# Six of nine modulation vectors move from TensorE to VectorE and GpSimd, their pieces loaded among the w_in and w_o chunks

## The chip, the cores and the metric

One core of one Trainium2 chip runs the whole program; everything is float32. The metric is the device time of one execution in microseconds (us). The engines are named as in the profile: PE is TensorE, DVE is VectorE, ACT is ScalarE, POOL is GpSimd, SP is SyncE, which issues nearly all loads.

## What is computed

A trunk of two layers over 256 tokens of 1024 channels. From one vector `c` each layer derives six modulation vectors of 1024 values, a shift, a scale and a gate for its mixer and the same for its expert layer:

```python
cs = jax.nn.silu(c)
for i in range(DEPTH):
    mod = cs @ w_mod[i] + b_mod[i]
    sh_m, sc_m, g_m, sh_f, sc_f, g_f = jnp.split(mod, 6, axis=-1)
    h = modulate(rmsnorm(x, norm_mix[i]), sh_m, sc_m)
    y = hybrid_ab(h, ...) if i % 2 == 0 else multiscale_pool(h, ...)
    x = x + g_m[:, None, :] * y
    h = modulate(rmsnorm(x, norm_ffn[i]), sh_f, sc_f)
    x = x + g_f[:, None, :] * hier_moe(h, ...)
return rmsnorm(x, norm_out)
```

So there are twelve vectors, called (layer, number) below: (0,0) and (0,1) are shift and scale of the first mixer, (0,2) its gate, (0,3), (0,4), (0,5) shift, scale and gate of the first expert layer, and (1,0) to (1,5) the same for the second layer. Each is a product of a 1024-vector with a 1024x1024 matrix, 4 MB of weights. The first mixer has sparse attention (an indexer, top 64 of the keys, eight heads) beside a gated spatial MLP, then the projection `w_o`; the second is a pooling mixer. The expert layer routes each token to two of 32 experts, whose weights are 96 MB per layer and are all loaded.

## The kernel before

The weights pass through `ring`, four slots of 2 MB. `plan` is the order of the 2 MB pieces: four pieces of (0,0) and (0,1), then `w_in` in the pieces qi, kv, (two pieces of (0,2)), q, v, u, then the two halves of `w_o`, then the pieces of (0,3), (0,4), (1,0) and (0,5). SP issues them in this order (L278), each when PE has used the piece four places ahead of it (`chunk_done`, one semaphore that counts pieces in PE's order). Every other load is behind it in the same queue. After the pieces come the expert weights, two experts at a time: a pair of slots holds gate and up weights, `dn_w` the down weights, and each load waits for the matmuls that read what it overwrites (L315 to L321). While the last experts of layer 0 run, the pieces of (1,1), (1,2) and then (1,3), (1,4), (1,5) are loaded.

PE computes a vector in `vector` (L446): every column of `cs` is broadcast to 32 columns of weights, so that four matmuls share the array, and a bias row is added by a matmul with a column of the identity. A gate vector then passes through ACT (`parts`, L836) and a second matmul (`gate`, L481) that sums its four parts; the others are copied to `stage` (L848) and turned on DVE (`scale_shift`, L1072). PE's order of work is written out: (0,0), (0,1), projection qi (L507), kv (L523), (0,2), key transposes (L529), indexer scores (L545), q, attention, v, the transposes of the probabilities, u, the spatial matmul (L637), values, `w_o` (L655); then `route(0)`: (0,3), (0,4), the transposes of the normed tokens (L495), the router (L667), (1,0), the counts, (0,5), the gather (L696); then the experts (L726, L738, L759, L773). After them (1,1), transposes, (1,2), the pooling mixer (L820), and `route(1)` with (1,3), (1,4), (1,5).

DVE carries the indexer: the weighted sum of the rectified scores (L1148, L1150), 8 rounds of `max` and `match_replace` per token block (L1169, L1170), then per unit of heads the distance term (L1211), mask and maximum (L1214), the division (L1226), and the GELU and layer norm of v (L1160, L1161, L1190 to L1199). ACT rectifies a unit of scores only when DVE has added the one before last (L893), copies `wsT` after the last of them (L898), and PE's projection q waits for that copy (L565). POOL has little: constants (L354 to L406), small loads, the power -1/2 of the norms (L367, L409, L411, L426), and the low parts of the tokens in `split_tokens` (L416).

## Time and profile before

| | us |
|---|---|
| median of 3 runs (776.96 to 777.67) | 777.55 |
| the profiled execution | 779.68 |
| its span from first to last instruction | 777.6 |

| engine | busy us | share of the span | instructions |
|---|---|---|---|
| PE | 679.7 | 87% | 4370 |
| DVE | 328.1 | 42% | 857 |
| ACT | 171.1 | 22% | 345 |
| POOL | 33.0 | 4% | 58 |

The chain of work that ended last is 49% PE and 44% DMA, of which 39% is `dn_w<-in_w_down`, the loads of the expert layers. The DMA engines are busy 85.5% of the span on SP's queue. A stretch that the chain gives to PE is one where PE had work without a gap; a stretch given to a DMA is one where PE stood until the load landed. Busy shares over the whole span mix stages that wait for different things, so the rows further down are read stage by stage.

### The profile page before, as it was taken

How to read it: one execution, taken by the hardware profiler on the slowest of the kernel's cores; microseconds unless marked ns; L12 is line 12 of the kernel's file. 1: busy time of each engine (PE TensorE's matmuls, PEld its weight loads, DVE VectorE, ACT ScalarE, POOL GpSimd, SP SyncE). 2: the span in 40 equal slices, each digit the busy share in tenths (PEclk: the TensorE clock that was granted, in tenths of full speed). 3: DMA queues.
4: the chain of work that ended last, by engine and by line, in shares of the span. 5: the costliest groups of instructions: out<-in, count | busy, mean ns of one | idle time of the engine just before them, and what ended most of it. 6: DMA issues, size and time to landing. Idle time of an engine off the chain costs nothing.

```text
span 777.6 us, 11606 instructions
## 1 busy us (share of the span) xinstructions
PE 679.7 (87%) x4370; PEld 386.2 (50%) x4370; DVE 328.1 (42%) x857; ACT 171.1 (22%) x345; POOL 33.0 (4%) x58
## 2 busy tenths in 40 slices
PE   4799998999998898889889879988988898898894
PEld 2285666435665444445445435456444454454442
DVE  1106973124634344334334485353443353343345
ACT  1003342012322122112113131223221121131121
POOL 3410000002000000000000000200000000000000
PEclk9999999998999999999999999889999999999998
DMA  8989333257989999999999999974799999999981
GB/s 334 351 300 352 108 109 109 107 227 315 399 359 398 420 421 422 422 422 421 422 421 424 414 399 410 384 303 178 308 422 420 423 422 421 422 422 422 422 361 54
DMA packets 49678, 269.63 MB, mean 347 GB/s; under 512 B 3796, under 2 KB 5908, under 8 KB 25072
## 3 DMA queue, kind: packets, MB, share of 16 engines
q1 hardware_dynamic: 48864, 268.22, 85.5%
q0 software_dynamic: 784, 1.00, 0.6%
q8 instruction: 20, 0.33, 0.2%
q14 instruction: 10, 0.08, 0.0%
HBM read 268.16 MB, written 1.05 MB: 346 GB/s over the span
## 4 chain that ended last, share of the span: by engine, by line
PE 49%; DMA 44%; ACT 2%; DVE 2%; issue 2%; SPq 1%; ACTq 0%; DVEq 0%
DMA dn_w<-in_w_down 39%; PE bank L759 15%; DMA ring<-in_w_mod 5%; PE bank L473 5%; PE bank L507 4%; PE bank L655 4%; PE bank L696 2%; PE bank L726 2%; PE bank L465 2%; PE bank L582 2%; PE bank L738 2%; PE bank L592 2%; PE bank L667 1%; PE bank L773 1%; PE bank L462 1%
## 5 line engine op out<-in xcount | busy, mean ns | idle before, releaser
L759 PE MATMUL bank<-dn_w,hT 128*64 128x512 f32 x480 | 109.5, 598 | 38.8 <-DMA dn_w<-in_w_down 38.8
L738 PE MATMUL bank<-ring,arena 128*64 128x256 f32 x1024 | 117.3, 382 | 10.3 <-DMA ring<-in_w_up 10.3
L726 PE MATMUL bank<-ring,arena 128*64 128x256 f32 x1024 | 117.6, 382 | 2.1 <-ACT arena L992 2.1
L1014 ACT CAST xn_parts<-arena 128x512 fp32r<-128x512 f32 x64 | 39.7, 620 | 275.1 <-DVE arena L1402 275.1
L738 PEld LDWEIGHTS bank<-ring,arena 128*64 128x64 f32 x1024 | 72.2, 137 | 54.4 <-DMA ring<-in_w_up 22.2
L1402 DVE SCALAR_TENSOR_TENSOR arena<-bank,hT,gates 128x512 f32<-128x512 f32 x64 | 48.0, 751 | 111.9 <-PE bank L759 111.9
L726 PEld LDWEIGHTS bank<-ring,arena 128*64 128x64 f32 x1024 | 71.5, 137 | 44.6 <-issue 13.0
L759 PEld LDWEIGHTS bank<-dn_w,hT 128*64 128x64 f32 x480 | 32.8, 136 | 102.4 <-issue 94.5
L773 PE MATMUL bank<-xn_parts,sel 128*128 128x512 f32 x256 | 66.5, 403 | 2.9 <-DVE xn_parts L1407 2.9
L1377 DVE SCALAR_TENSOR_TENSOR hT<-hT,bank 128x256 f32<-128x256 f32 x32 | 19.1, 598 | 101.7 <-PE bank L738 101.7
L473 PE MATMUL bank<-ring,cs 128*32 128x256 f32 x512 | 54.5, 590 | 2.1 <-DMA ring<-in_w_mod 2.1
L773 PEld LDWEIGHTS bank<-xn_parts,sel 128*128 128x128 f32 x256 | 45.9, 188 | 13.2 <-DVE xn_parts L1407 4.7
L1407 DVE TENSOR_TENSOR xn_parts<-arena,xn_parts 128x512 fp32r<-128x512 f32 x64 | 44.0, 687 | 2.9
L992 ACT COPY arena<-arena 128x512 f32 x68 | 42.0, 625 | 5.3 <-issue 1.9
L1372 DVE SCALAR_TENSOR_TENSOR hT<-hT,bank 128x256 f32<-128x256 f32 x32 | 13.5, 421 | 57.7 <-ACT hT L999 57.5
L473 PEld LDWEIGHTS bank<-ring,cs 128*32 128x32 f32 x512 | 18.2, 128 | 36.3 <-issue 31.0
L507 PE MATMUL bank<-hT,ring 128*128 128x256 f32 x128 | 29.8, 396 | 2.8 <-ACT hT L867 2.8
L999 ACT ACTIVATE hT<-bank 128x256 f32<-128x256 f32 x32 | 12.3, 383 | 83.6 <-PE bank L726 83.6
L507 PEld LDWEIGHTS bank<-hT,ring 128*128 128x128 f32 x128 | 25.3, 199 | 8.1 <-ACT hT L867 3.8
L655 PE MATMUL bank<-ring,xn 128*128 128x512 f32 x64 | 27.7, 593 | 1.6 <-issue 1.6
L465 PE MATMUL bank<-ring,cs 128*32 128x512 f32 x128 | 23.5, 664 | 0.0
L860 ACT ACTIVATE arena<-x_res 128x1024 f32<-128x1024 f32 x10 | 10.5, 1054 | 53.9 <-DVE x_res L1106 44.9
(258 smaller groups left out, 617.1 us busy)
## 6 DMA issues: line engine op xcount, KB each, us to landing
ring<-in_w_gate SPq DMA_DIRECT2D x32, 2048.0 KB, 14.3
ring<-in_w_up SPq DMA_DIRECT2D x32, 2048.0 KB, 18.8
dn_w<-in_w_down SPq DMA_DIRECT2D x30, 2048.0 KB, 11.0
ring<-in_w_mod SPq DMA_DIRECT2D x24, 2048.0 KB, 14.6
ring<-in_w_in SPq DMA_DIRECT2D x4, 2048.0 KB, 9.8
ring<-in_w_o SPq DMA_DIRECT2D x2, 2048.0 KB, 11.4
ring<-in_w_down SPq DMA_DIRECT2D x2, 2048.0 KB, 15.2
x_res<-in_x SPq DMA_DIRECT2D x2, 512.0 KB, 4.2
```

The costliest lines, as they stand in the source:

```text
L465: ins = pe.matmul(bank[half][32 * q:32 * q + 32, :], cs[:, 2, k:k + 1].to_broadcast([P, 32]), w[:, q, at], start=not last, stop=last)
L473: ins = pe.matmul(to, cs[:, 2, k:k + 1].to_broadcast([P, 32]), by_quadrant(w[:, kk, :], q, natural), start=not last and kk == 0, stop=False)
L507: ins = pe.matmul(bank[banks[m // 2]][:, (m % 2) * T:(m % 2 + 1) * T], w[:, k, m * P:(m + 1) * P], hT[:, k, :], start=(k == 0), stop=(k == ...
L655: ins = pe.matmul(bank[(3, 4, 6, 7)[2 * half + t]][:, :], catT[:, k, t * P:(t + 1) * P], w[:, k, :], start=(k == 0), stop=(k == KT - 1))
L726: ins = pe.matmul(bank[2][h * WIN:(h + 1) * WIN, 0:FE], xw[:, b, h, k, :], w[:, h, 0, k, :], start=(k == 0), stop=(k == KT - 1))
L738: ins = pe.matmul(bank[3][h * WIN:(h + 1) * WIN, 0:FE], xw[:, b, h, k, :], w[:, h, 1, k, :], start=(k == 0), stop=(k == KT - 1))
L759: ins = pe.matmul(bank[n][h * WIN:(h + 1) * WIN, :], actT[:, t, h * WIN:(h + 1) * WIN], w[:, h, t, n * HALF:(n + 1) * HALF], start=(t == 0 ...
L773: ins = pe.matmul(bank[4 + 2 * n + t][:, :], sel[:, b, t * P:(t + 1) * P], xn_parts[:, part, b, n * HALF:(n + 1) * HALF], start=(isinstanc ...
L992: ins = act.copy(xw[:, b, h], xgT[:, :, bass.ds(start, WIN)])
L1014: act.copy(xn_parts[:, 0, b, at], y_s[:, b, at]).then_inc(e["y_hi"], 1)
L1402: stt(y_s[:, b, at], bank[n][:, :], slot_gate[:, b:b + 1], gates[:, 2 * l + 1, at], ALU.mult, ALU.mult).then_inc(e["y_kept"], 1)
L1407: tt(xn_parts[:, 1, b, at], y_s[:, b, at], xn_parts[:, 0, b, at].bitcast(F32), ALU.subtract).then_inc(e["y_lo"], 1)
```

## The change

`vector` is no longer called for six vectors. (0,2), (0,4), (0,3) are summed on DVE (`accumulate`), (0,5), (1,1), (1,2) on POOL (`scaled`, `added`), both on full 128 partitions with the weights where they lie in the ring; PE then only sums over the partitions (`reduce`). (0,0), (0,1), (1,0), (1,3), (1,4), (1,5) stay on PE. The pieces of the six are placed in the order of loads among the `w_in` and `w_o` pieces, `slots` gives each its slot, and `slot_freed` makes SP wait for the engine that used the piece before it in that slot. The pieces loaded during the last experts of layer 0 are now those of (1,3), (1,4), (1,5) alone. `vector((1, 3))` moves ahead of the pooling mixer. On POOL the constants come ahead of the small loads, and the sums of its vectors lie before, between and after the two powers of the first mixer.

```diff
+        def halves(vec):
+            return [("mod", 2 * mods.index(vec) + part) for part in range(2)]
+
+        BY_DVE = ((0, 2), (0, 4), (0, 3))
+        BY_POOL = ((0, 5), (1, 1), (1, 2))
+        (m2a, m2b), (m4a, m4b), (m3a, m3b), (m5a, m5b) = halves((0, 2)), halves((0, 4)), halves((0, 3)), halves((0, 5))
+        (n1a, n1b), (n2a, n2b), (n0a, n0b) = halves((1, 1)), halves((1, 2)), halves((1, 0))
+        front = [(("mod", 0), 0), (("mod", 1), 1), (("mod", 2), 2), (("mod", 3), 3),
+                 (("in", "qi"), 0), (m2a, 1), (("in", "kv"), 3), (m2b, 2), (m5a, 1), (m5b, 2), (("in", "q"), 0), (("in", "v"), 3),
+                 (n1a, 1), (n1b, 2), (("in", "u"), 0), (n2a, 1), (n2b, 2), (("out", 0), 3), (m4a, 1), (("out", 1), 0), (m4b, 2),
+                 (m3a, 1), (m3b, 2), (n0a, 1), (n0b, 2)]
+        middle = [(m, slot) for m, slot in zip(halves((1, 3)) + halves((1, 4)) + halves((1, 5)), (0, 1, 2, 3, 0, 1))]
+        plan, slots = zip(*front, *middle)
+        FIRST = len(front)
+        PAIRS = (((0, 3), (1, 2)), ((2, 3), (0, 1)))
+        place = {key: n for n, key in enumerate(plan)}
+        by_dve = [key for vec in BY_DVE for key in halves(vec)]
+        by_pool = [key for vec in BY_POOL for key in halves(vec)]
+        by_pe = [("mod", 0), ("mod", 1), ("mod", 2), ("mod", 3), ("in", "qi"), ("in", "kv"), ("in", "q"), ("in", "v"), ("in", "u"),
+                 ("out", 0), ("out", 1), n0a, n0b] + [m for m, slot in middle]
+        assert sorted(by_dve + by_pool + by_pe, key=str) == sorted(plan, key=str)
...
         def slot_of(n):
-
-            return n % CH if n < FIRST else (1, 3, 0, 2)[(n - FIRST) % CH]
+            return slots[n]
+
+        def slot_freed(eng, n):
+
+            last = max(i for i in range(n) if slot_of(i) == slot_of(n))
+            key = plan[last]
+            if key in by_dve:
+                eng.wait_ge(S["dve_used"], by_dve.index(key) + 1)
+            elif key in by_pool:
+                eng.wait_ge(S["pool_used"], by_pool.index(key) + 1)
+            else:
+                eng.wait_ge(S["chunk_done"], chunk_no[key] + 1)
-        turns = [mods[m // 2] for kind, m in plan if kind == "mod" and m % 2 == 0]
+        turns = [(0, 0), (0, 1), (0, 2), (0, 4), (0, 3), (1, 0), (0, 5), (1, 1), (1, 2), (1, 3), (1, 4), (1, 5)]
         columns = [v for v in turns if v not in GATE]
         gated = [v for v in turns if v in GATE]
+
+        vec_sum = {v: gates[:, n, :] for v, n in GATE.items()}
+        vec_sum[0, 4], vec_sum[0, 3], vec_sum[1, 1] = ar(2048, D), ar(3072, D), gates[:, 3, :]
+        reduced = [v for v in turns if v in BY_DVE + BY_POOL and v not in GATE]
 
 # SP
             for n in range(FIRST):
                 if n >= CH:
-                    sp.wait_ge(S["chunk_done"], n - CH + 1)
...
-                sp.wait_ge(S["chunk_done"], base + 2)
+                sp.wait_ge(S["chunk_done"], chunk_no[("out", 1) if l == 0 else ("mod", 21)] + 1)
                 gate_load(l, 0, 0)
+                sp.wait_ge(S["chunk_done"], chunk_no[("mod", 13) if l == 0 else ("mod", 23)] + 1)
                 gate_load(l, 1, 2)
                 up_load(l, 1, 2)
 # POOL, after the small loads
+            pool.wait_ge(S["csb_ready"], 1)
+
+            def scaled(vec, part):
+
+                n = place[halves(vec)[part]]
+                pool.wait_ge(chunk_in[slot_of(n)], arrivals(n))
+                w = mod_at(n)
+                for kk in range(KT // 2):
+                    k = part * (KT // 2) + kk
+                    ins = pool.tensor_scalar(w[:, kk, :], w[:, kk, :], cs[:, 2, k:k + 1], None, ALU.mult)
+                done(ins)
+
+            def added(vec, part):
+
+                w, acc = mod_at(place[halves(vec)[part]]), vec_sum[vec]
+                done(pool.tensor_tensor(w[:, 0:2, :], w[:, 0:2, :], w[:, 2:4, :], ALU.add))
+                if part == 0:
+                    pool.tensor_tensor(acc, w[:, 0, :], w[:, 1, :], ALU.add).then_inc(S["pool_used"], 1)
+                else:
+                    done(pool.tensor_tensor(w[:, 0, :], w[:, 0, :], w[:, 1, :], ALU.add))
+                    pool.tensor_tensor(acc, acc, w[:, 0, :], ALU.add).then_inc(S["pool_used"], 1)
+
+            scaled((0, 5), 0)
             pool.wait_ge(S["kv_ms"], 1)
             pool.tensor_tensor(stat[:, 10:12], stat[:, 8:10], mhalf[:], ALU.pow).then_inc(S["kv_inv"], 1)
+            added((0, 5), 0)
+            scaled((0, 5), 1), added((0, 5), 1)
+            scaled((1, 1), 0), added((1, 1), 0)
+            scaled((1, 1), 1), added((1, 1), 1)
+            scaled((1, 2), 0), added((1, 2), 0)
             pool.wait_ge(S["ln_ms"], 1)
             pool.tensor_tensor(stat[:, 18:20], stat[:, 16:18], mhalf[:], ALU.pow).then_inc(S["ln_inv"], 1)
+            scaled((1, 2), 1), added((1, 2), 1)
+
             def split_tokens(l):
 
                 pool.wait_ge(S["xn_part1"], l + 1)
 # PE
+            def reduce(vec):
+
+                if vec in BY_DVE:
+                    pe.wait_ge(S["dve_used"], 2 * BY_DVE.index(vec) + 2)
+                else:
+                    pe.wait_ge(S["pool_used"], 2 * BY_POOL.index(vec) + 2)
+                free_banks(pe, vec)
+                r = ident[:, BIAS_ROW[vec]:BIAS_ROW[vec] + 1]
+                if vec in GATE:
+                    for half in range(2):
+                        at = slice(half * HALF, (half + 1) * HALF)
+                        ins = pe.matmul(bank[half][:, :], ones[:], vec_sum[vec][:, at], start=True, stop=vec in BY_DVE)
+                        if vec in BY_POOL:
+                            ins = pe.matmul(bank[half][:, :], r.to_broadcast([P, P]), rows[:, at], start=False, stop=True)
+                        ins.then_inc(S["gate_done"], 1)
+                else:
+                    natural, b = vec in NATURAL, banks_of(vec)[0]
+                    to = [bank[b][32 * q:32 * q + 32, 0:KT * 32].rearrange("p (k i) -> p k i", k=KT) for q in range(4)]
+                    for q in range(4):
+                        ins = pe.matmul(to[q], ones[:, 0:32], by_quadrant(vec_sum[vec], q, natural), start=True, stop=vec in BY_DVE)
+                    for q in range(4 if vec in BY_POOL else 0):
+                        ins = pe.matmul(to[q], r.to_broadcast([P, 32]), by_quadrant(rows[:, :], q, natural), start=False, stop=True)
+                    ins.then_inc(S["reduced"], 1)
+
-            vector((0, 2))
...
-            gate((0, 2), 0), gate((0, 2), 1)
+            reduce((0, 2))
...
-                vector((l, 3)), vector((l, 4))
+                if l == 0:
+                    reduce((0, 4)), reduce((0, 3))
+                else:
+                    vector((1, 4))
...
-                    vector((0, 5))
+                    reduce((0, 5))
...
-                    gate((0, 5), 0), gate((0, 5), 1)
 
...
-            vector((1, 1))
+            reduce((1, 1)), reduce((1, 2))
             turn(2, natural=True)
-            vector((1, 2))
-            gate((1, 2), 0), gate((1, 2), 1)
+            vector((1, 3))
 # DVE
+            def accumulate(vec):
+
+                acc, r = vec_sum[vec], BIAS_ROW[vec]
+                dve.wait_ge(S["early_in"], 16 * EARLY)
+                done(ts(acc, rows[:, :], ident[:, r:r + 1], None, ALU.mult))
+                for part in range(2):
+                    n = place[halves(vec)[part]]
+                    dve.wait_ge(chunk_in[slot_of(n)], arrivals(n))
+                    for kk in range(KT // 2):
+                        k = part * (KT // 2) + kk
+                        w = mod_at(n)[:, kk, :]
+                        ins = stt(acc, w, cs[:, 2, k:k + 1], acc, ALU.mult, ALU.add)
+                        if kk < KT // 2 - 1:
+                            done(ins)
+                    ins.then_inc(S["dve_used"], 1)
+                    dve.wait_ge(S["dve_used"], 2 * BY_DVE.index(vec) + part + 1)
+
...
+            accumulate((0, 2))
...
+            accumulate((0, 4)), accumulate((0, 3))
```

ACT's `keep_column` waits for `reduced` where a vector is summed elsewhere; (0,2), (0,5) and (1,2) skip `parts` and only pass `keep_gate`.

## Rows read from the trace of the kernel before

**Rows 1.** Busy time by stage; columns: stretch, length, busy us of each engine, clock, DMA.
```profile
213.50:446.60 233.10, 207.74 (x1432) 113.59 (x1432) 93.44 (x206) 49.62 (x97) 0.00 (x0) 1.00 1.00 414
446.60:530.50 83.90, 71.77 (x469) 41.46 (x470) 49.23 (x143) 22.06 (x40) 6.04 (x4) 0.92 0.88 349
530.50:777.60 247.10, 211.53 (x1444) 115.70 (x1444) 100.55 (x219) 51.63 (x100) 1.11 (x2) 0.99 0.89 369
```

**Rows 2.** Chain of waits, start of both expert stages; columns: start us, length us, what.
```profile
201.54 8.16 PE bank L696 x32
213.51 3.67 PE bank L726 x32
232.53 8.77 DMA dn_w<-in_w_down
...
516.17 10.74 PE bank L696 x32
530.49 3.67 PE bank L726 x32
549.51 8.85 DMA dn_w<-in_w_down
```

**Rows 3.** PE in order of time: start us, length us, line, operation, count.
```profile
118.18 1.95 PE L637 MATMUL bank<-arena 128*128 128x128 f32 x16
134.58 27.70 PE L655 MATMUL bank<-ring,xn 128*128 128x512 f32 x64 [1.64 <-issue]
162.22 7.54 PE L473 MATMUL bank<-ring,cs 128*32 128x256 f32 x64
178.90 1.28 PE L495 MATMUL bank<-ident,xn 128*128 128x128 f32 x9
...
492.60 2.06 PE L495 MATMUL bank<-ident,xn 128*128 128x128 f32 x16
```

**Rows 4.** DVE in order of time, where PE or the next stage waits for it.
```profile
114.97 1.00 DVE L1199 TENSOR_SCALAR arena<-arena,rt,stat 128x512 f32<-128x512 f32 x2
...
166.08 1.42 DVE L1069 TENSOR_SCALAR xn<-x_res,stat 128x1024 f32<-128x1024 f32 x2 [0.80 <-POOL stat L367]
...
485.46 1.42 DVE L1069 TENSOR_SCALAR xn<-x_res,stat 128x1024 f32<-128x1024 f32 x2 [0.81 <-POOL stat L367]
```

**Rows 5.** PE in order of time: first matmuls of vector (0,2), first transpose after it.
```profile
57.79 1.92 PE L465 MATMUL bank<-ring,cs 128*32 128x512 f32 x16
63.05 0.44 PE L529 MATMUL bank<-ident,arena 128*128 128x128 f32 x2
```

**Rows 6.** Busy time by stage again, one short stretch; last two columns DMA share, GB/s.
```profile
50.00:52.00 2.00, 2.00 (x11) 1.77 (x10) 0.00 (x0) 0.00 (x0) 0.00 (x0) 1.00 0.63 250
```

**Rows 7.** DVE from 61.5 to 115 us by line and shape: busy us, mean ns.
```profile
L1150 DVE SCALAR_TENSOR_TENSOR arena<-arena,w 128x256 f32<-128x256 f32 x7 | 3.4, 485 | 0.3
L1214 DVE CUSTOM_DVE_ANT_0 dn_w<-dn_w,arena 128x256 f32<-128x256 f32 x8 | 3.1, 422 | 0.1
L1226 DVE TENSOR_SCALAR dn_w<-dn_w,asum 128x256 f32<-128x256 f32 x8 | 2.5, 350 | 0.1
L1161 DVE TENSOR_TENSOR dn_w<-dn_w,arena 128x1024 f32<-128x1024 f32 x1 | 1.2, 1226 | 0.0
```

**Rows 8.** GpSimd in order of time: the same subtractions, a fill, a power.
```profile
2.79 0.96 POOL L369 MEMSET rows<- 128x1024 f32 x1 [0.15 <-POOL pick L361]
58.80 0.72 POOL L409 TENSOR_TENSOR stat<-stat,mhalf 128x2 f32<-128x2 f32 x1 [15.66 <-DVE stat L1123]
184.08 4.64 POOL L416 TENSOR_TENSOR xn_parts<-xn,xn_parts 128x1024 fp32r<-128x1024 f32 x2 [18.04 <-ACT xn_parts L966]
497.78 4.66 POOL L416 TENSOR_TENSOR xn_parts<-xn,xn_parts 128x1024 fp32r<-128x1024 f32 x2 [12.35 <-ACT xn_parts L966]
```

**Rows 9.** DVE beside the two long GpSimd subtractions, in order of time.
```profile
188.52 0.23 DVE L1260 TENSOR_TENSOR rt<-rt 128x8 f32<-128x8 f32 x1
...
501.93 0.53 DVE L1260 TENSOR_TENSOR rt<-rt 128x8 f32<-128x8 f32 x1
```

More of the change, by code:

```diff
@@ L161, in trunk @@
         mods = [(l, v) for l in range(L) for v in range(6)]
-        plan = [("mod", m) for m in range(4)] + [("in", "qi"), ("in", "kv"), ("mod", 4), ("mod", 5), ("in", "q"), ("in", "v"),
-                ("in", "u"), ("out", 0), ("out", 1)]
-        plan += [("mod", m) for m in (6, 7, 8, 9, 12, 13, 10, 11, *range(14, 24))]
-        FIRST = plan.index(("mod", 14))
-        chunk_no = {key: n for n, key in enumerate(plan)}
+        def halves(vec):
+            return [("mod", 2 * mods.index(vec) + part) for part in range(2)]
@@ L376, in _ @@
             power(0)
+            done(pool.memset(before[:], 1.0))
+            done(pool.affine_select(out=before[:], in_=before[:], compare_op=ALU.is_gt, fill=0.0, base=0,
+                                    pattern=[[1, P]], channel_multiplier=-1))
+            done(pool.iota(slot_no[:], [[1, SLOTS]], base=0, channel_multiplier=0, allow_small_or_imprecise_dtypes=True))
+            for t in range(TT):
+                done(pool.iota(dist[:, t, :], [[-1, T]], base=t * P, channel_multiplier=1,
+                               allow_small_or_imprecise_dtypes=True))
+            done(pool.iota(edge[:], [[1, 16]], base=1, channel_multiplier=0, allow_small_or_imprecise_dtypes=True))
+            done(pool.iota(rank[:], [[-1, 8]], base=8, channel_multiplier=0, allow_small_or_imprecise_dtypes=True))
+            done(pool.iota(lane[:], [[0, 1]], base=0, channel_multiplier=1, allow_small_or_imprecise_dtypes=True))
+            done(pool.tensor_scalar(lane[WIN:P, :], lane[WIN:P, :], -float(WIN), None, ALU.add))
+            pool.memset(win_i[0:1, PASSES * NE:PASSES * NE + 2], 0)
+            done(pool.iota(eid_i[:], [[0, PASSES], [1, NE]], base=0, channel_multiplier=0))
+            pool.sem_inc(S["consts"], 1)
             pool.wait_ge(chunk_in[slot_of(3)], arrivals(3))
@@ L392, in _ @@
                     pool.dma_start(dst, src).then_inc(S["late_in"], 16)
-            done(pool.memset(before[:], 1.0))
-            done(pool.affine_select(out=before[:], in_=before[:], compare_op=ALU.is_gt, fill=0.0, base=0,
-                                    pattern=[[1, P]], channel_multiplier=-1))
-            done(pool.iota(slot_no[:], [[1, SLOTS]], base=0, channel_multiplier=0, allow_small_or_imprecise_dtypes=True))
-            for t in range(TT):
-                done(pool.iota(dist[:, t, :], [[-1, T]], base=t * P, channel_multiplier=1,
-                               allow_small_or_imprecise_dtypes=True))
```

44 lines of the change are left out of this document (19 added, 25 removed).

## The prediction, made before the changed kernel was run

> **What bounds the kernel now.** I read the busy times by stage first, then the chain of waits, then PE's and DVE's instructions in order of time around the places where they meet. The kernel is four stretches: a front to 213.5 us, the experts of layer 0 (233.1 us), a middle of 83.9 us, and from 530.5 us the experts of layer 1 with the end (247.1 us) [rows 1]. Both expert stages run at 1.00 and 0.89 of the DMA engines. Their length hangs on when PE starts them: the first `dn_w` load that PE stands for is issued at 232.53 and 549.51, both 19.0 us after the first expert matmul at 213.51 and 530.49 [rows 2], for it waits for matmuls of the first expert, not for earlier loads. So loading the first experts earlier earns nothing, and I hold both stages fixed. What can move is the start of each, in the front and in the middle.
>
> In the front PE is the bound almost throughout. After `w_o` (134.58 to 162.3) PE works on (0,3) and (0,4) from 162.22 and starts the transposes at 178.90 [rows 3]; DVE had the normed tokens ready at 166.08 + 1.42 = 167.5 [rows 4]. In the middle the transposes start at 492.60 [rows 3], the tokens are ready at 486.9 [rows 4]. In both, PE's vectors are the later of two.
>
> **What the change gives: three places.** (a) After `w_o` only two sums over partitions remain (eight matmuls with 32 columns, under 2 us), beside the residual, squares and norm, which take 167.5 - 162.3 = 5.2 us. The transposes start 5.2 us after `w_o` instead of 16.6: 11.4 us. What is late next is the norm. (b) (0,5) no longer stands before the gather at 201.54 [rows 2], but the selection matrix that the gather also needs was ready only about 0.4 us earlier: 0.4. (c) In the middle, (1,3) is done while DVE pools, (1,1) and (1,2) shrink to sums, and after the mixer only (1,4) is left, 8.3 us that end before the tokens are ready: 492.6 - 486.9 = 5.7 us. PE stands 3.4 and 2.6 us in (a) and (c), and a pause costs clock: the gather takes 8.16 us without a pause and 10.74 after one of 3 us [rows 2]. I charge 1.0 and 0.7. Sum of the gains: 11.4 + 0.4 + 5.7 - 1.7 = 15.8.
>
> (d) (0,2) leaves PE after kv, 57.79 to 63.05 [rows 5]. Behind it hides the key norm: DVE's mean, POOL's power, DVE's scaling, ready at about 60.2. Now POOL has to reach its power. The four pieces behind `w_in` kv carry the same bytes in another order, and before they had landed at about 51.2 (0.63 of the stretch from 50 to 52) [rows 6]. So the second piece of (0,2) lands there. DVE adds four pieces of 1024 columns at 1.23 us and 0.04 between them [rows 7], 5.1 us, and is done at 56.3, ahead of the key norm at 58.5: this vector costs nothing. The first piece of (0,5) takes 2.1 MB at some 400 GB/s, 5.2 us, and lands at 56.4. POOL scales it before its power.
>
> **The price on POOL.** Each half vector is four scalings of 128x1024, one sum of 128x2048, one of 128x1024, and in the second half one more. Two subtractions of 128x1024 take 4.64, so one sum is 2.3 and the double one 4.6 [rows 8]. A scaling isn't in the trace. Below it is bounded by a fill of the same shape, 0.96, above by the two-input 2.3 [rows 8]; one input and one output stand nearer to the fill, and I take 1.1, with 0.96 and 2.3 kept for the range. Halves are then 11.3 and 13.7 us. The Trainium skill (GPSIMD Engine Reference, Engine selection) calls one-input work on GpSimd roughly line-rate; the trace shows no such instruction of this size, and by that rule the scalings would be a little under my 1.1.
>
> The first scalings end at 60.8, the power follows to 61.5, the keys are ready at 62.3 against 63.05: of the 5.3 us about 0.7 is left. Then POOL has four and a half more halves before the next power, the one of v's layer norm: from 56.4, 61.3 us of sums, 0.7 for the first power and 1.0 of waits end at 119.4. Today the spatial matmul L637 starts at 118.18 [rows 3], DVE having scaled v at 114.97 + 1.00 [rows 4]. Undisturbed POOL would give 0.7 + 1.3 us later, 121.4: a loss of 3 us.
>
> **POOL and DVE get in each other's way.** Twice a small DVE operation with two inputs in SBUF lies beside a long subtraction on POOL. L1260 at 188.52 takes 0.23 and ends at 188.75; POOL ends at 188.72. At 501.93 the same shape takes 0.53 and ends at 502.46; POOL ends at 502.44 [rows 8, 9]. The next of its kind takes 0.17. A reduction with one input just before takes its usual 0.16 beside POOL. So a DVE operation with two SBUF inputs stands until POOL's whole instruction is over. This is the rule of the Trainium skill (SBUF — State Buffer, on engine and DMA ports), an exclusive lock held for a whole instruction, against two-input and 2-port DVE operations; here the trace agrees, and the sum below is what it makes of POOL's work.
>
> From 61.5 to ln_ms DVE has such work in plenty: 14 weighted score sums (5.9 us), 16 mask-and-maximum (5.0), 16 divisions (4.3; one input, so no row shows whether these stand too, and I count them) and some 20 others, altogether 21.1 us [rows 7]. The selection, 15 us of one-input work like the reduction that was not held up, I count as free.
>
> One end, DVE first: DVE's next operation follows 0.04 us after the last and POOL gets in only in longer gaps. Then POOL is held back by the 21.1 us and reaches the power at 119.4 + 21.1 = 140.5; v is ready at 142.5, 24 us later than L637 wants it. DVE's own delays (one rest of a POOL instruction per burst, about ten of them) hide behind that. Add 2 for the GELU of u against the last half, and 2.6 of clock after a 24 us pause [rows 2]: the front is 28.6 later by `w_o`.
>
> Other end, they take turns: each of the 16 operations of the score sums waits for one POOL instruction: 0.7 + 2.3 + 4.4 + 4.6 + 2.3 + 2.3 + 4.4 + 4.6 + 2.3 + 2.2 = 30 us. ACT rectifies behind DVE, copies `wsT` behind that, and PE's projection q waits for the copy, so PE stands too. The half that is left meets mask and maximum: 9 more. Less 2 of slack, plus 1 behind the second power and 2.6 of clock: 40.
>
> Net: 28.6 - 15.8 = +12.8, or 40 - 15.8 = +24. I take +16.5, nearer to the first, because the gap inside a DVE chain is 0.04 us. The later loads stay hidden: u's piece comes after POOL's use of the fourth piece, some 20 us before PE needs it; the last pieces of (0,4) and (0,3) reach DVE during the 27.7 us of `w_o`.
>
> The sum is made against the profiled execution, 779.68 with its span of 777.6 and 2.1 around it; that is 2.1 above the median of the runs, 777.55, to which I apply the difference: 777.55 + 16.5 = 794. Own range of this case 786 to 806.
>
> **Rivals.** (1) No lock where it matters: POOL's instructions let DVE through, or the two seldom meet. Then the front loses 3 - 0.7 and 0 of clock, the gains stay: -15.8 + 2.4 = -13.4, 764 us. For it speaks that the lock is shown by two instances of 0.06 and 0.36 us only, both against a two-input POOL instruction; against it, that both ends agree to 0.03 us. Chance 0.32. (2) The scaling costs what a sum costs: 20 scalings by 1.2 more, +24 at the second power. Without the lock 764 + 24 = 788, with it 812 or more. Against it: nothing in the trace with one input on POOL is that slow. Chance 0.08. (3) The two effects nearly cancel: POOL is late, but meets less than half of DVE's operations, 11 of 21 us and 3 lost: 774 to 779. Chance 0.08. (4) The ring holds up the front: a piece of `w_in` is late since SP waits in order for POOL. It needs POOL to be 20 us later than in my sum; it is part of (2).
>
> **How the numbers follow.** The forecast has 0.52. What can be told from no change is 0.2%, 1.6 us. Faster: rival 1 and half of rival 3, 0.36. Same: 0.04. Slower: 0.60. The range takes in the faster side: 762 to 806 leaves out a tenth at each end.
>
> **What would show it.** Right: L637 at 140 or later, with PE standing before it on DVE and that on POOL's power; L1150, L1214 or L1226 with means well above 485, 422 and 350 ns beside POOL; POOL's scalings near 1.1 us; `w_o` to transposes in 5 us; the middle about 78 us; the expert stages 233 and 247. Wrong: score sums ending at 73 and L637 before 123, then the time is near 764; or a middle as long as now, then (c) failed.

## The result, and the profile after

The changed kernel takes 816.41 us (median of four runs, 813.32 to 817.66) against 777.61 (776.96 to 779.55) beside it: ratio 1.049, 95% interval 1.046 to 1.052. That is +38.8 us where the forecast was +16.5 and its range ended at +28.5; the direction is right, the size is not. The profiled execution of the changed kernel has a span of 815.9 us, 38.3 above the span before.

First the busy time by stage, as in [rows 1], with the front cut once more at 182 and 218 (columns: stretch, length, busy us and instructions of PE, PEld, DVE, ACT, POOL, granted clock, DMA share, GB/s).

```profile
60.00:100.00 40.00, 26.98 (x114) 20.60 (x115) 24.12 (x62) 5.82 (x10) 39.60 (x15) 0.68 0.57 211
100.00:182.00 82.00, 50.50 (x190) 33.37 (x188) 58.87 (x113) 18.75 (x52) 78.40 (x27) 0.83 0.50 183
182.00:218.00 36.00, 32.60 (x80) 13.60 (x80) 29.22 (x30) 2.83 (x6) 0.72 (x1) 0.91 0.82 308
255.00:493.00 238.00, 212.12 (x1456) 115.63 (x1452) 97.47 (x213) 50.37 (x99) 0.00 (x0) 0.99 0.97 402
568.00:815.00 247.00, 211.61 (x1444) 115.82 (x1444) 100.95 (x219) 52.48 (x101) 1.10 (x2) 0.99 0.89 370
```

The expert stages are as long as before (from the first to the last expert matmul 236.5 us for 236.6 in layer 0, from the first expert matmul to the end of the program 247.2 for 247.1 in layer 1) and nearly as full of transfers. From 60 to 182 us GpSimd is busy for 118.0 of 122 us, PE for 77.5. Now PE in order of time, the rows that answer to [rows 3] and [rows 5] (start, length, line, operation, and in brackets the pause before it and what ended it).

```profile
71.16 0.69 PE L611 MATMUL bank<-ident,arena 128*128 128x128 f32 x2 [15.23 <-DVE arena L1234]
159.94 3.75 PE L719 MATMUL bank<-arena 128*128 128x128 f32 x16 [18.36 <-DVE xn L1335]
182.38 6.17 PE L737 MATMUL bank<-ring,xn 128*128 128x512 f32 x7 [5.46 <-issue]
218.29 2.10 PE L578 MATMUL bank<-ident,xn 128*128 128x128 f32 x11 [3.32 <-DVE xn L1154]
254.79 1.52 PE L809 MATMUL bank<-ring,arena 128*64 128x256 f32 x12 [2.03 <-ACT arena L1079]
529.72 3.56 PE L578 MATMUL bank<-ident,xn 128*128 128x128 f32 x16 [2.54 <-DVE xn L1154]
568.65 1.73 PE L809 MATMUL bank<-ring,arena 128*64 128x256 f32 x14 [1.79 <-ACT arena L1079]
```

Against [rows 2, 3, 5] that is +8.1 at the key transposes (71.16 for 63.05), +41.8 at the spatial matmul (159.94 for 118.18), +47.8 at `w_o` (182.38 for 134.58), +39.4 at the token transposes, +41.3 and +38.2 at the experts. The whole loss arises before `w_o`. Behind it 8.4 come back up to the token transposes, 1.9 are lost again up to the experts, and the middle brings 3.1.

GpSimd by line and shape, 40 to 182 us (busy us, mean ns), answers to [rows 8]:

```profile
L446 POOL TENSOR_SCALAR ring<-ring,cs 128x1024 f32<-128x1024 f32 x24 | 68.8, 2881 | 18.3 <-DMA ring<-in_w_mod 18.3
L452 POOL TENSOR_TENSOR ring<-ring 128x2048 f32<-128x2048 f32 x6 | 27.2, 4532 | 0.4
L454 POOL TENSOR_TENSOR gates<-ring 128x1024 f32<-128x1024 f32 x3 | 7.0, 2340 | 0.2
```

A scaling takes 2.88 us, not 1.1; the sums are as priced. Next DVE beside it, 60 to 182 us, for [rows 7], where the same groups have 350, 485 ns:

```profile
L1329 DVE TENSOR_SCALAR dn_w<-dn_w,asum 128x256 f32<-128x256 f32 x8 | 13.2, 1688 | 0.2
L1253 DVE SCALAR_TENSOR_TENSOR arena<-arena,w 128x256 f32<-128x256 f32 x7 | 4.9, 695 | 0.2
```

In order of time it can be seen what a division stands for: first DVE, then GpSimd, both from 128.7.

```profile
128.72 7.09 DVE L1329 TENSOR_SCALAR dn_w<-dn_w,asum 128x256 f32<-128x256 f32 x2
135.91 3.43 DVE L1329 TENSOR_SCALAR dn_w<-dn_w,asum 128x256 f32<-128x256 f32 x2
```

```profile
128.72 4.52 POOL L452 TENSOR_TENSOR ring<-ring 128x2048 f32<-128x2048 f32 x1
133.31 2.34 POOL L456 TENSOR_TENSOR ring<-ring 128x1024 f32<-128x1024 f32 x1
135.73 2.34 POOL L457 TENSOR_TENSOR gates<-gates,ring 128x1024 f32<-128x1024 f32 x1
```

Two divisions of 0.35 us last 7.09: each stands for one whole sum, and GpSimd's sums keep their lengths here. Where VectorE's instruction is long, GpSimd stands too. At 173.76 VectorE multiplies two inputs of 128x1024, 1.23 us by itself; again first DVE, then GpSimd:

```profile
173.76 3.25 DVE L1264 TENSOR_TENSOR dn_w<-dn_w,arena 128x1024 f32<-128x1024 f32 x1
```

```profile
173.25 2.67 POOL L456 TENSOR_TENSOR ring<-ring 128x1024 f32<-128x1024 f32 x1
176.00 3.20 POOL L457 TENSOR_TENSOR gates<-gates,ring 128x1024 f32<-128x1024 f32 x1
```

VectorE's product ends at 177.01, 1.1 us after GpSimd's L456; GpSimd's L457, begun at 176.00, takes 3.20 instead of 2.34. Up to the second power GpSimd loses little in this way: against the shortest rows of each kind (11.31 for four scalings, 4.5 and 2.34 for the sums) I estimate 1.3 us.

### The profile page after: what moved, and what is told of

Its sections match the earlier page's. It is cut to its first block, busy times and chain, and to the rows that moved or that the text cites. A ratio compares the mean times of both kernels' runs of the same rounds, so it can differ in the third digit from the quotient of the medians.

```text
span 815.9 us, 11109 instructions
## 1 busy us (share of the span) xinstructions
PE 670.2 (82%) x4086; PEld 389.6 (48%) x4086; DVE 393.5 (48%) x884; ACT 167.8 (21%) x339; POOL 152.4 (19%) x97
## 3 DMA queue, kind: packets, MB, share of 16 engines
HBM read 268.16 MB, written 1.05 MB: 330 GB/s over the span
## 4 chain that ended last, share of the span: by engine, by line
DMA 41%; PE 36%; POOL 12%; DVE 5%; issue 2%; ACT 2%; SPq 0%; ACTq 0%; DVEq 0%; POOLq 0%
DMA dn_w<-in_w_down 37%; PE bank L842 15%; POOL ring L446 7%; PE bank L737 4%; DMA ring<-in_w_mod 4%; POOL ring L452 3%; PE bank L532 2%; PE bank L781 2%; PE bank L809 2%; PE bank L821 2%; PE bank L752 2%; PE bank L578 1%; PE bank L856 1%; ACT arena L945 1%; PE bank L674 1%
## 5 line engine op out<-in xcount | busy, mean ns | idle before, releaser
L842 PE MATMUL bank<-dn_w,hT 128*64 128x512 f32 x480 | 111.2, 605 | 36.8 <-DMA dn_w<-in_w_down 36.8
L809 PEld LDWEIGHTS bank<-ring,arena 128*64 128x64 f32 x1024 | 71.6, 137 | 45.9 <-issue 13.7
L446 POOL TENSOR_SCALAR ring<-ring,cs 128x1024 f32<-128x1024 f32 x24 | 68.8, 2881 | 18.3 <-DMA ring<-in_w_mod 18.3
L396 POOL TENSOR_TENSOR stat<-stat,mhalf 128x2 f32<-128x2 f32 x4 | 2.8, 707 | 337.7 <-DVE stat L1151 337.7
L1079 ACT COPY arena<-arena 128x512 f32 x68 | 42.2, 624 | 6.7 <-issue 4.0
L532 PE MATMUL bank<-ring,cs 128*32 128x256 f32 x320 | 35.5, 608 | 2.2 <-DMA ring<-in_w_mod 2.2
L737 PE MATMUL bank<-ring,xn 128*128 128x512 f32 x64 | 30.6, 643 | 5.5 <-issue 5.5
L590 PE MATMUL bank<-hT,ring 128*128 128x256 f32 x128 | 28.0, 380 | 2.8 <-ACT hT L952 2.8
## 6 DMA issues: line engine op xcount, KB each, us to landing
ring<-in_w_down SPq DMA_DIRECT2D x2, 2048.0 KB, 15.2
```

Source lines behind the costliest of these rows:

```text
L446: ins = pool.tensor_scalar(w[:, kk, :], w[:, kk, :], cs[:, 2, k:k + 1], None, ALU.mult)
L532: ins = pe.matmul(to, cs[:, 2, k:k + 1].to_broadcast([P, 32]), by_quadrant(w[:, kk, :], q, natural), start=not last and kk == 0, stop=False)
L590: ins = pe.matmul(bank[banks[m // 2]][:, (m % 2) * T:(m % 2 + 1) * T], w[:, k, m * P:(m + 1) * P], hT[:, k, :], start=(k == 0), stop=(k == ...
L737: ins = pe.matmul(bank[(3, 4, 6, 7)[2 * half + t]][:, :], catT[:, k, t * P:(t + 1) * P], w[:, k, :], start=(k == 0), stop=(k == KT - 1))
L809: ins = pe.matmul(bank[2][h * WIN:(h + 1) * WIN, 0:FE], xw[:, b, h, k, :], w[:, h, 0, k, :], start=(k == 0), stop=(k == KT - 1))
L842: ins = pe.matmul(bank[n][h * WIN:(h + 1) * WIN, :], actT[:, t, h * WIN:(h + 1) * WIN], w[:, h, t, n * HALF:(n + 1) * HALF], start=(t == 0 ...
```

## The experiments

Each ratio is against the kernel before, run on the same chip beside it.

**1. VectorE's three vectors alone.** GpSimd gets nothing; (0,5), (1,1) and (1,2) stay on PE.

```
-BY_POOL = ((0, 5), (1, 1), (1, 2))
+BY_POOL = ()
+    (m2b, 2), (("in", "q"), 1), (("in", "v"), 0), (m4a, 2), (("in", "u"), 3), (("out", 0), 1), (m4b, 0), (m3a, 2), (("out", 1), 3), (m3b, 0), ...
```

> The three vectors of DVE stay moved, the three of POOL go back to PE with their pieces at their old places; POOL has its old work again. Theory 1 (the whole loss is on POOL's side: long scalings that the two powers and the ring wait for): DVE's part is a gain of its own. The keys are ready at about 60.3 instead of 63.05 (2.7 us), the transposes start 5.2 us after w_o instead of 16.6 (11.4 us), less 1 of clock; the middle is unchanged at 83.9. 777.6 - 13 = 764 to 766. Theory 2 (DVE's sums themselves hold the front up, for their pieces come late or DVE is late for the residual): 772 or more, with DVE busy when w_o ends.

777.98 us (772.48 to 781.11), ratio 1.000 (0.997 to 1.003). The 38.8 us are gone, so they belong to what GpSimd had been given, but the gain of theory 1 isn't there either (764 to 766). In the trace `w_o` starts at 133.47, 1.1 us before [rows 3], and the experts at 211.51, 2.0 before [rows 2]. PE stops inside `w_o` (first line below), since its second half is loaded late: SyncE issued the load of m3a only when VectorE had used m4a, 34.5 us after the load before it, and `w_o`'s half stood behind that (the two SPq lines).

```profile
154.13 2.08 PE L730 MATMUL bank<-ring,xn 128*128 128x512 f32 x2 [6.70 <-DMA ring<-in_w_o]
```

```profile
105.29 34.53 SPq L296 DMA_DIRECT2D ring<-in_w_mod  x2
139.87 1.42 SPq L299 DMA_DIRECT2D ring<-in_w_o  x1
```

**2. Both powers on ScalarE.** The sums stay on GpSimd; the powers of kv and of v become a logarithm and an exponential on ACT.

```
-pool.tensor_tensor(stat[:, 18:20], stat[:, 16:18], mhalf[:], ALU.pow)
+act.activation(stat[:, 28:30], stat[:, 16:18], ACT.Ln)
+act.activation(stat[:, 18:20], stat[:, 28:30], ACT.Exp, scale=-0.5)
...
```

> The changed kernel, but the powers -1/2 of the key norm and of v's norm are taken on ACT (logarithm, then exponential), so nothing waits for POOL there; POOL's sums are unchanged. Theory 1a (the two powers are where POOL's length costs): PE no longer stands 15 us before the key transposes and 18 us before the spatial matmul, and the time falls by 25 to 30, to 787 to 792. Theory 1b (POOL's length costs wherever the ring asks for it: the pieces of (0,3) and (0,4) wait for slots that POOL frees at 179): the spatial matmul comes 20 us or more earlier, but DVE's last sum still ends near 208 and the transposes at 215 to 218; 811 to 815. Theory 2 (the shared port stretches DVE's chain): the spatial matmul stays at 150 or later.

814.39 us (812.47 to 815.81), ratio 1.047 (1.045 to 1.050). The keys come 5.0 us after PE wants them instead of 15.2, yet the spatial matmul is hardly sooner:

```profile
158.78 3.75 PE L715 MATMUL bank<-arena 128*128 128x128 f32 x16 [17.03 <-DVE xn L1340]
```

On the way to it, at 150.15, VectorE has a `TENSOR_SCALAR` of 128x2 that takes 3.87 us, and behind it two of 128x512 that take 3.90 together, 1.0 with GpSimd idle. Without its powers GpSimd makes PE late by what it does to VectorE, as theory 2 has it; VectorE's sums end at 207.4, as theory 1b has it.

**3. GpSimd's operations alone.** The kernel before, with single operations on scratch in an idle stretch of GpSimd.

```
+done(pool.tensor_scalar(probe, probe, cs[:, 2, 0:1], None, ALU.mult))
+done(pool.tensor_scalar(probe, probe, 0.5, None, ALU.mult))
...
+done(pool.tensor_copy(probe2, probe))
+done(pool.tensor_tensor(probe, probe, cs[:, 2, 0:1].to_broadcast([P, D]), ALU.mult))
+done(pool.tensor_tensor(probe, probe, probe2, ALU.mult))
```

> The kernel before, with eight extra POOL instructions in POOL's idle time before 29 us: scaling 128x1024 by a column of scalars, by a constant, 128x512 by a column, a copy, a product with a broadcast column, a product of two tiles. Theory 1 (the scaling is dear by itself, whatever DVE does): 2.83 for the column even with DVE idle; the constant tells whether it is the column that costs (about 1.1 if so), or the operation (2.8). Theory 2 (it was 2.83 because DVE was in its way): 1.1 to 1.3 here. Product of two tiles 2.3 by either. Time of the whole within 1 us of before.

Time 780.3 (one run; the kernel before beside it took 775.21 to 779.71). By line and shape (busy us, mean ns):

```profile
L381 POOL TENSOR_SCALAR arena<-arena,cs 128x1024 f32<-128x1024 f32 x1 | 3.2, 3172 | 0.1
L382 POOL TENSOR_SCALAR arena<-arena 128x1024 f32<-128x1024 f32 x1 | 2.8, 2776 | 0.1
L385 POOL TENSOR_TENSOR arena<-arena,cs 128x1024 f32<-128x1024 f32 x1 | 1.9, 1895 | 0.1
L386 POOL TENSOR_TENSOR arena<-arena 128x1024 f32<-128x1024 f32 x1 | 2.4, 2413 | 0.1
L384 POOL COPY arena<-arena 128x1024 f32<-128x1024 f32 x1 | 1.0, 1045 | 0.1
```

The scaling is dear by itself and dearer than the product of two tiles; a copy of the same size costs a third of it. No VectorE instruction lies beside the scaling by a constant (2.78). The first line holds a wait: VectorE's scaling of `xn` (L1079) runs until 12.44 and GpSimd's had begun at 11.99, so that about 2.8 are left for the column too.

**4. The scaling as a product of two inputs.**

```
-ins = pool.tensor_scalar(w[:, kk, :], w[:, kk, :], cs[:, 2, k:k + 1], None, ALU.mult)
+ins = pool.tensor_tensor(w[:, kk, :], w[:, kk, :], cs[:, 2, k:k + 1].to_broadcast([P, D]), ALU.mult)
```

> The changed kernel, with each of POOL's scalings written as a product with a broadcast column (two inputs). Theory 1 (length alone): at 2.3 instead of 2.83 each the second power comes 20 x 0.5 = 10 us earlier and the time falls by about 10, to 806. Theory 2 (the port): a two-input POOL instruction holds DVE's two-input work for its whole length where the scaling held it for only 1.25 of 2.83 us, so DVE's score sums take 25 us or more instead of 12, and the time is 816 or more although POOL is faster.

824.73 us (822.26 to 826.42), ratio 1.059 (1.057 to 1.062): GpSimd needs 0.9 us less for each of 24 scalings, and the kernel is 8.3 slower than the changed one. VectorE's score sums pay, 2.4 us each instead of 0.35 and 0.49:

```profile
L1253 DVE SCALAR_TENSOR_TENSOR arena<-arena,w 128x256 f32<-128x256 f32 x7 | 17.0, 2435 | 0.2
L1253 DVE SCALAR_TENSOR_TENSOR arena<-arena,w 128x128 f32<-128x128 f32 x7 | 16.8, 2400 | 0.2
```

GpSimd isn't what is late here: ahead of the second power it stands 20.8 us for VectorE's variance of v. So VectorE's waits cost by themselves, and they grew while GpSimd's work became shorter.

```profile
165.09 0.70 POOL L468 TENSOR_TENSOR stat<-stat,mhalf 128x2 f32<-128x2 f32 x1 [20.76 <-DVE stat L1297]
```

**5. No work on GpSimd.** The six pieces are loaded, waited for and given back; the sums are one column wide, and (0,5), (1,1) and (1,2) are left out of the result.

```
-pool.tensor_scalar(w[:, kk, :], w[:, kk, :], ...)
+pool.tensor_scalar(w[:, kk, 0:1], w[:, kk, 0:1], ...)
...
```

> The changed kernel with GpSimd's sums cut to one column (its six pieces are still loaded, waited for and given back; modulation vectors (0, 5), (1, 1) and (1, 2) are left out of the result, and with them the routing of the second layer's tokens is another, which can move the experts of that layer by some us). GpSimd takes no time and holds nobody. Both theories say that all of the loss goes: the experts of layer 0 start at 200 to 206 instead of 254.8, median 764 to 772. If it is over 780, the loss has a part outside GpSimd (the plan of the ring, VectorE's own sums).

767.66 us (764.99 to 768.90), ratio 0.986 (0.982 to 0.990). With GpSimd's work the kernel is 48.8 us longer; the rest of the change brings 10.0. The experts of layer 0 start at 210.16, not at the 200 to 206 expected: 44.6 of the 48.8 lie before them. The other 4 lie behind, in a part where this kernel also leaves three vectors out of its result, so that they aren't shown to be GpSimd's.

**6. Length without operands.** As many us of memsets.

```
+for fill in range(3):
+    done(pool.memset(w[:, kk, :], 0.0))
...
```

> The changed kernel with each of GpSimd's instructions of the sums replaced by memsets that last about as long together (three 128x1024 for a scaling, six or eight for the sums of a piece; 17 to 20 us a piece). The three vectors are left out of the result as in the kernel before this one in the list, and compare it with that one. GpSimd is as late with its pieces and with the two powers, but its instructions read nothing and have no second operand. Theory 2 (GpSimd's sums cost by what they do to VectorE's instructions beside them): VectorE's score sums stay at 350 ns for 128x128 and its divisions at 350 for 128x256, the experts of layer 0 start at most 12 us later than with GpSimd idle (the two powers), median at most 784. Rival 1 (they cost by their length: pieces given back late, powers late): median 806 to 818, as the changed kernel. If a memset holds VectorE too, divisions and score sums are longer here as well, and the time lies with the rival's; then the rows of VectorE tell which it is.

817.92 us (817.35 and more; one of the four runs took 1315.5, which is not explained), ratio 1.051 (1.046 to 1.056). The time is the rival's, but it isn't reached by the changed kernel's path. The score sums have 352 and 485 ns again, as [rows 7]; the scores of the second tokens (98.66) are 7 us later than with GpSimd idle, where in the changed kernel (102.44) they are 11. The divisions still wait, one memset each: pairs of 0.35 us last

```profile
117.75 1.97 DVE L1326 TENSOR_SCALAR dn_w<-dn_w,asum 128x256 f32<-128x256 f32 x2
```

and what makes PE late is now the power, which stands behind 20 us of each piece (sums of DVE's waits, then of PE's: total, times, longest):

```profile
DVE stat L1297 <- POOL stat L465: 29.0, 1, 29.0
DVE arena L1231 <- POOL stat L458: 11.9, 1, 11.9
```

```profile
PE bank L716 <- DVE xn L1332: 35.3, 1, 35.3
```

**7. Length without operands and without powers.** Memsets as in experiment 6, powers on ScalarE as in experiment 2.

> The changed kernel with memsets in place of GpSimd's sums (the three vectors left out of the result) and also both powers of kv and v taken by ScalarE (logarithm and exponential): GpSimd is as long over its six pieces, but nobody waits for a power, and its instructions have no operands. With the powers on GpSimd this kernel took 817.9. Theory A (the powers were what remained of the loss): w_o starts at 138 to 146, median 776 to 788. Theory B (the length has a second way to the end: the pieces of (0, 4) and (0, 3) stand in the ring behind GpSimd's, VectorE can't start on them before 182, and the residual needs them): w_o starts at 146 or sooner, yet VectorE's sums still run from about 182 to 208 and the transposes come at 213 to 218; median 810 to 818.

815.06 us (814.08 to 817.56), ratio 1.047 (1.044 to 1.050): theory B, with one miss: `w_o` starts at 153.9, not at 146 or sooner. The spatial matmul is at 129.5, but the pieces in the ring aren't there. `w_o` waits for both its halves, and the sums that the residual needs end at 207.8 as before:

```profile
153.89 15.68 PE L730 MATMUL bank<-ring,xn 128*128 128x512 f32 x32 [7.68 <-DMA ring<-in_w_o]
174.91 15.43 PE L730 MATMUL bank<-ring,xn 128*128 128x512 f32 x32 [5.33 <-DMA ring<-in_w_o]
```

```profile
189.47 5.24 DVE L1197 SCALAR_TENSOR_TENSOR arena<-ring,cs,arena 128x1024 f32<-128x1024 f32 x4 [14.56 <-DMA ring<-in_w_mod]
202.53 5.25 DVE L1197 SCALAR_TENSOR_TENSOR arena<-ring,cs,arena 128x1024 f32<-128x1024 f32 x4 [1.75 <-DMA ring<-in_w_mod]
```

**8. Shorter sums.** Experiment 2 with each addition in pieces of 512 columns.

> The kernel with real sums and the powers on ScalarE (814.4), with each of GpSimd's additions cut into pieces of 512 columns (a 128x2048 of 4.5 us becomes four, a 128x1024 of 2.4 us two; about 1.3 us each). If VectorE and GpSimd take turns instruction by instruction, no instruction of VectorE waits over 1.6 us beside an addition (before: 3.5 each for the two divisions at 128.5), the spatial matmul moves from 158.8 to 145 or sooner, and the six pieces are done 3 to 8 us later than 178.5. The median is then set by the pieces alone: 812 to 822. If it is the work moved and not the instruction that is traded, the spatial matmul stays at 155 or later.

821.64 us (817.55 to 823.90), ratio 1.054 (1.051 to 1.058). The spatial matmul moves from 158.8 to 140.4, and no VectorE instruction stands longer beside a piece of a sum than about 1.1 us: they take turns by instruction. (The two divisions of 7.09 take 2.15 at most, but they lie beside scalings now.) GpSimd ends at 188.4, 9.9 later than in experiment 2, more than the 3 to 8 expected, and the token transposes go with it, 217.2 to 224.2. A part of the 9.9 is GpSimd's own waiting: pieces of a sum that take 1.27 take 2.24 beside VectorE's two-input instructions of 128x1024.

```profile
158.10 2.24 POOL L453 TENSOR_TENSOR ring<-ring 128x512 f32<-128x512 f32 x1
```

**9. `w_o` ahead in the queue.** Experiment 1 with one reordering.

```
-(("in", "u"), 3), (("out", 0), 1), (m4b, 0), (m3a, 2), (("out", 1), 3), (m3b, 0), (n0a, 2), (n0b, 1), (m5a, 0), (m5b, 3)
+(("in", "u"), 3), (("out", 0), 1), (("out", 1), 0), (m4b, 3), (m3a, 2), (m3b, 3), (n0a, 2), (n0b, 1), (m5a, 3), (m5b, 0)
```

> The kernel in which VectorE alone takes its three vectors (778), with one thing moved: w_o's second half stands in SyncE's queue directly behind its first half, in the slot that the v chunk leaves, ahead of the pieces that wait for VectorE to add up (0, 4). In that kernel's trace TensorE waited 6.7 us for this half, and VectorE's sums of (0, 3) 3.3 and 5.3 us for their pieces. Theory 1 (the gain of VectorE's three vectors was real and was given back in the ring's order): w_o is done 6.7 us sooner, and what follows it by up to 9; median 768 to 771. Rival (what VectorE adds up delays its own later work, whatever the order): the experts start no sooner and the median stays at 776 to 780.

771.05 us (766.46 to 774.73), ratio 0.989 (0.984 to 0.994); the same kernel in a later series on the same chip (expectation below) 774.06 (770.35 to 774.60), ratio 0.995 (0.992 to 0.997). `w_o` runs through without a pause. The experts start at 210.37 and, in the later series, at 207.95, against 211.51 in experiment 1: 1.1 and 3.6 us sooner, where up to 9 were expected. So a part of the gain is back, 3.2 and 6.6 us by the medians against the kernel before; the two series differ by 3.0.

> The kernel with w_o's second half ahead in the queue once more, to stand on the same chip beside the one before: 769 to 774.

**10. Filling for PE's pauses.** What is left over shows in the kernel of experiment 5, which has the same three vectors on VectorE (PE in order of time):

```profile
62.81 7.69 PE L626 MATMUL bank<-arena 64*128 64x128 f32 x32 [0.58 <-DVE arena L1237]
172.67 3.68 PE L577 MATMUL bank<-ident,xn 128*128 128x128 f32 x16 [4.90 <-DVE xn L1153]
177.60 7.01 PE L751 MATMUL bank<-wroute,hT 128*128 128x36 f32 x32 [1.26 <-issue]
```

PE has also stood 4.9 us before the key transposes, just ahead of the scores (first line). Behind both pauses the granted clock is 0.50, the lower level of 1.2 GHz: 32 score matmuls take 7.69 (28 of them took 3.52 before, at 1.00), the transposes 3.68 for 2.05, the routing 7.01 for 5.33. The first try put (0,2) back and moved (1,0) ahead of the transposes.

```
-BY_DVE = ((0, 2), (0, 4), (0, 3))
+BY_DVE = ((0, 4), (0, 3))
...
-    reduce((0, 4)), reduce((0, 3))
+    reduce((0, 4)), reduce((0, 3)), vector((1, 0))
```

> The kernel with w_o's second half ahead in the queue (771.05), with two pieces of TensorE's work put back as filling: vector (0, 2) is TensorE's again, between kv and the keys as before the change, and (1, 0) is taken before the token transposes instead of behind the routing. Without them TensorE stood still for 4.9 and 5.8 us, and what followed ran at half the clock: the 32 score matmuls in 7.69 us (28 of them took 3.52 before), the transposes in 3.67 (2.05), the routing in 7.01 (5.33). Theory (the clock took back part of the gain): scores, transposes and routing run at the short times again, w_o starts at 134.6 instead of 137.4, the experts of layer 0 start at 206 to 208 instead of 210.4; median 766 to 769. Rival (the clock costs nothing that counts, and putting back 5 us of columns costs as much): 770.5 to 774.

774.50 us (771.90 to 777.75), ratio 0.996 (0.994 to 0.998), on another chip than experiment 9; by the ratios no gain over its kernel: the rival, though half a microsecond above its range. `w_o` starts at 132.25, but the experts at 209.9. The filling took the pause away in one place and left it in the next: (1,0) waits 3.12 us for its bank, and (0,5), alone behind the routing, runs slow and on the chain from 190.23 to 197.84, behind a pause of 5.2 us.

The second puts only (0,2) back.

> The kernel with w_o's second half ahead in the queue, with vector (0, 2) alone put back on TensorE, between kv and the keys; (1, 0) stands behind the routing again. In the kernel with both put back w_o started at 132.25 (5.2 sooner than without either), but (1, 0) waited 3.1 us for its bank and (0, 5), left alone behind the routing, ran at half the clock on the chain, and the experts started at 209.9. Theory (the clock took part of the gain at the keys, and the 5 us gained there reach the experts if nothing else is moved): w_o at 132 to 133, transposes at 167 to 169, experts of layer 0 at 204 to 206, median 4 to 6 below the kernel run beside it (w_o first). Rival (what is won at the keys is lost again before the experts, whatever the filling): experts at 209 or later, within 2 of the kernel beside it.

769.50 us (764.88 to 771.08), ratio 0.989 (0.986 to 0.992), 4.6 below experiment 9's kernel on the same chip. Scores and `w_o`:

```profile
63.89 3.52 PE L621 MATMUL bank<-arena 64*128 64x128 f32 x28 [0.59 <-DVE arena L1237]
134.17 27.70 PE L731 MATMUL bank<-ring,xn 128*128 128x512 f32 x64 [1.64 <-issue]
205.17 3.67 PE L805 MATMUL bank<-ring,arena 128*64 128x256 f32 x32 [0.31 <-ACT arena L1077]
```

`w_o` starts at 134.17 (132 to 133 was expected) and the experts at 205.2, 8.3 us before [rows 2]. The second pause is still there: the token transposes take 3.68 behind 5.5 us. This kernel, with two vectors on VectorE and none on GpSimd, is 1.1% faster than the one before and, by the two ratios, 5.7% faster than the changed one.

## Why the prediction was right or wrong

**The scaling's price: wrong, and the step that failed.** "One input and one output stand nearer to the fill, and I take 1.1", between 0.96 and 2.3. It is 2.88, above the upper bound. I had taken one kind of instruction (a fill) as the measure for another because both have few inputs, and bounded it by a sum because that reads more. Experiment 3 shows that on GpSimd the number of inputs doesn't order the prices. Twenty scalings lie before v's power: 20 x (2.88 - 1.1) = 35.6 us. What came is nearest to rival 2 with the lock ("with it 812 or more", at a price of 2.3), which I gave a chance of at most 0.08 and left out of my range; "nothing in the trace with one input on POOL is that slow" was no evidence, for the trace had none of that size. The Trainium skill (GPSIMD Engine Reference, Engine selection) calls one-input work roughly line-rate; the copy of 1.05 fits that, the scaling of 2.8 doesn't.

**"GpSimd is held back by the 21.1 us": wrong.** It was busy 118.0 of 122 us in instructions of nearly undisturbed length. My undisturbed 119.4 plus 35.6, plus 1.9 since the first piece landed at 58.3 instead of 56.4, is 156.9; the power came at 156.57. The forecast's 140.5 was 16 us early: 35.6 too little for the price and 21.1 too much for a delay that didn't occur, two errors of which one hid a part of the other.

**"They take turns", the other end: right.** DVE waits for one GpSimd instruction at a time, and GpSimd for one of DVE's, which is seldom seen because most of DVE's are short (3.20 for 2.34 us at 176.00 is the longest). I had leaned to the wrong end because of DVE's gaps of 0.04 us. The Trainium skill (SBUF — State Buffer, Who interferes with whom) says more than I used: against DVE's two-input operations only a GpSimd instruction that reads is in the way, against `tensor_scalar` in a mode that uses both ports any, and whoever comes second waits. Experiments 4 and 6 agree with both halves: two-input score sums 2.4 us beside products, 0.49 beside memsets, and divisions 1.0 beside memsets. I had counted the divisions without knowing. Its rule that the lock lasts for the whole instruction holds for sums (3.5 us a division), not for a scaling: a score sum that met one 0.14 us after its start took 1.12 us, and the next four in its 2.85 us went freely.

**Rival 4, the ring, which I had put aside as "part of 2": it was real, and "The later loads stay hidden" was wrong.** Its condition was GpSimd 20 us later than in my sum. That sum ends the pieces at 140.5 + 0.7 + 13.7 = 154.9; they ended at 179.2. SyncE stood for GpSimd's sums six times, 97.8 us in all (waits of the queue in the changed kernel from 50 to 215 us: total, times, longest; 2.2 in experiment 5):

```profile
SPq L296 <- POOL gates L457: 49.2, 3, 20.8
SPq L296 <- POOL gates L454: 48.6, 3, 17.6
```

The front has three ways from GpSimd to its end: the wait of DVE's instructions, the powers, and the ring, in which `w_o` and the pieces of (0,4) and (0,3) stand behind GpSimd's. Here is what each kernel leaves of them (us):

| | port | powers | pieces late | spatial matmul | DVE's sums end | experts 0 | median |
|---|---|---|---|---|---|---|---|
| changed | yes | yes | yes | 159.9 | 208.3 | 254.8 | 816.4 |
| exp. 2 | yes | no | yes | 158.8 | 207.4 | 252.6 | 814.4 |
| exp. 6 | part | yes | yes | 164.2 | 207.7 | 254.5 | 817.9 |
| exp. 7 | part | no | yes | 129.5 | 207.8 | 254.4 | 815.1 |
| exp. 5 | no | no | no | 121.7 | 163.1 | 210.2 | 767.7 |

Here "port" is what GpSimd's instructions do to VectorE's, "part" that only the divisions and their like wait. Without the powers the port brings the spatial matmul to 158.8, with the port in part the powers bring it to 164.2, and with the port in part and no powers the late pieces bring the experts to 254.4. Three causes lie side by side, and taking one or two away shows next to nothing. The powers and the pieces follow from some 118 us of sums on GpSimd between 58.3 and 179.2: a scaling at 1.1 would have ended the pieces 24 x 1.78 = 43 us sooner (an estimate; not tried). The port doesn't follow from the length: experiment 4 had shorter scalings and longer waits. How much the port would have cost with scalings at 1.1 stays open.

**The gains.** (a) `w_o` to transposes 5.3 us against 16.6: right (213.0 to 218.3). (b) 0.4: too small to be seen. (c) Behind the pooling mixer 5.6 (before 25.4 from the mixer to the transposes, after 19.8) against 5.7: right; but the sum of (1,2) shares a bank with (1,1) and waits for its copy, so the first transposes of the middle come 244.9 us behind the experts' start instead of 242.0: 2.9 given back, 1.5 won at the mixer. The middle brought 3.1, not 5.0.

**The clock was mis-sized.** I charged 1.7 behind two pauses of the gains. From the transposes to the experts it is 36.5 against 34.6 after `w_o` and 38.9 against 37.9 in the middle, 2.9 together, and 2.9 more in `w_o` itself (50.7 late at its end, 47.8 at its start), where the granted clock is 0.52 for the first 6.2 us behind a pause of 5.5.

**(d), "this vector costs nothing": wrong in three traces of four in which GpSimd had nothing to sum, and hidden under the rest.** VectorE's sum of (0,2) ends at 58.4 in the changed kernel, not at 56.3, still in time for the key norm. But PE, without (0,2), stands. With GpSimd idle `w_o` starts 3.5 us later than before (138.09), because PE pauses for 4.9 us and takes 7.69 us for the scores. It depends on the pause: in experiment 9's two traces (4.3 and 3.8 us) the scores take 7.69 too and `w_o` starts at 137.44 and 136.05, in experiment 1 (2.9 us) they take 6.47 and it starts at 133.47, before [rows 3]. Experiment 10 puts the vector back: `w_o` at 134.17, 1.9 before the kernel beside it, and 4.6 less in all. Rival 1's 764 lies 3.7 below experiment 5's 767.7 and at the low edge of its interval (0.982 to 0.990).

Redone: +47.8 at `w_o`, +2.9 in it, -11.3 behind it, +1.9 clock, -3.1 in the middle: +38.2, the spans' 38.3.

## What to carry to other kernels

Price an instruction by one of its own kind on its own engine, or, if there is none, keep the upper end open; a shorter operand list isn't a shorter instruction. Before an engine is filled up, list what else hangs on it (small steps behind its queue, ring slots that it frees, the neighbour that shares its port), and expect that removing one of these shows nothing while the others stand. Work taken off PE inside a pause can cost the clock of what follows: the vector that filled the wait for the keys was free where it was.
